# Each sample scored over its own 272 keys, latent queries over 128 rows, one copy and two tile turns at other places

## What is computed

```python
q_lat = jnp.einsum('bthn,rhn->bthr', q_nope, w_uk)
o_lat = mla_attend(q_lat, q_rope,
                   jnp.concatenate([ckv_past, ckv_new], axis=1),
                   jnp.concatenate([krope_past, kr_new], axis=1), None)
# in mla_attend: s = (q_lat . ckv + q_rope . krope) * ATTN_SCALE; p = softmax(s); p @ ckv
```

## Time and profile before

| | us |
|---|---|
| median of 3 runs | 776.85 (776.73 to 777.43) |
| the profiled execution | 776.64 |
| its span, first to last instruction | 774.8 |
| PE busy | 761.0 (98%), 3767 matrix instructions |
| DVE busy | 565.1 (73%) |
| ACT busy | 422.4 (55%) |
| POOL busy | 65.3 (8%) |
| chain that ended last | PE 90%, DVE 5%, ACT 3%, issue 1% |

### The profile page before, as it was taken

How to read it: one execution, slowest core, us unless ns; L and a number is a source line. 1 busy time by engine, 2 the same in 40 slices (tenths; PEclk the granted TensorE clock), 3 DMA queues, 4 the chain that set the end, 5 groups by cost and what they waited for, 6 DMA issues and landing times.

```text
span 774.8 us, 10544 instructions
## 1 busy us (share of the span) xinstructions
PE 761.0 (98%) x3767; PEld 605.5 (78%) x3767; DVE 565.1 (73%) x1092; ACT 422.4 (55%) x982; POOL 65.3 (8%) x114
## 2 busy tenths in 40 slices
PE   8999999999999999999999999999999999999995
PEld 7899877777777588888888988787777766888874
DVE  3459989877877985636463799898778789656477
ACT  3865656764446743263365485557544558223564
POOL 1400123210000400000000010232000000000000
PEclk9999999999999999999999999999999999999998
DMA  8822222100000353412281322221000005341203
GB/s 269 257 77 82 83 71 85 39 29 27 2 27 17 97 200 125 134 56 82 59 280 52 99 81 77 66 59 28 28 27 28 1 28 176 96 136 59 87 19 136
DMA packets 45833, 65.54 MB, mean 85 GB/s; under 512 B 12590, under 2 KB 24714, under 8 KB 45766
## 3 DMA queue, kind: packets, MB, share of 16 engines
q1 hardware_dynamic: 41946, 58.45, 24.0%
q0 software_dynamic: 3776, 6.40, 2.9%
q10 hardware_dynamic: 60, 0.02, 0.0%
HBM read 57.87 MB, written 7.18 MB: 84 GB/s over the span
## 4 chain that ended last, share of the span: by engine, by line
PE 90%; DVE 5%; ACT 3%; issue 1%; POOL 0%; DVEq 0%; ACTq 0%; POOLq 0%
PE acc L660 19%; PE acc L666 19%; PE acc L663 19%; PE sharedT L584 5%; PE acc L796 4%; PE sharedS L871 4%; PE sharedO L885 4%; PE sharedT L858 3%; PE sharedO L584 2%; PE sharedS L584 2%; PE sharedS L844 1%; PE sharedS L845 1%; PE sharedO L832 1%; DVE H L1804 1%; PE sharedS L852 1%
## 5 line engine op out<-in xcount | busy, mean ns | idle before, releaser
L660 PE MATMUL acc<-WHI,XHI 128*128 128x512 f32 (+1 forms) x710 | 309.2, 435 | 1.0 <-ACT WHI L1051 0.5
L666 PE MATMUL acc<-WHI,XLO 128*128 128x512 f32 (+1 forms) x710 | 274.6, 387 | 0.0
L663 PE MATMUL acc<-WLO,XHI 128*128 128x512 f32 (+1 forms) x710 | 274.3, 386 | 0.3 <-DVE WLO L1475 0.3
L1545 DVE SCALAR_TENSOR_TENSOR VT<-UX,CWT,VT 128x640 f32<-128x640 f32 x240 | 211.4, 882 | 4.6
L660 PEld LDWEIGHTS acc<-WHI,XHI 128*128 128x128 f32 x710 | 133.7, 188 | 33.0 <-issue 8.1
L663 PEld LDWEIGHTS acc<-WLO,XHI 128*128 128x128 f32 x710 | 133.9, 189 | 30.5 <-issue 8.1
L1475 DVE SCALAR_TENSOR_TENSOR WLO<-WR,GT,WHI 128x512 fp32r<-128x512 f32 (+1 forms) x142 | 98.6, 736 | 78.6 <-ACT WHI L1051 77.7
L666 PEld LDWEIGHTS acc<-WHI,XLO 128*128 128x128 f32 x710 | 133.3, 188 | 26.1
L1051 ACT ACTIVATE WHI<-WR,GT 128x512 fp32r<-128x512 f32 (+1 forms) x142 | 93.4, 709 | 91.3 <-PE acc L666 91.1
L1267 ACT ACTIVATE SB<-SB,NBIAS 128x384 f32<-128x384 f32 (+1 forms) x80 | 46.0, 574 | 39.7 <-DVE NBIAS L1599 39.1
L1051 ACT ACTIVATE PT<-sharedT 128x384 f32<-128x384 f32 (+1 forms) x80 | 35.7, 447 | 44.1 <-PE sharedT L584 43.2
(11 more groups left out here) (204 smaller groups left out, 872.5 us busy)
## 6 DMA issues: line engine op xcount, KB each, us to landing
WR<-in_w_in_dram SPq DMA_DIRECT2D x32, 256.0 KB, 3.1
WR<-in_w_in_dram SPq DMA_DIRECT2D x16, 512.0 KB, 3.6
WR<-in_w_out_dram SPq DMA_DIRECT2D x16, 512.0 KB, 3.7
WR<-in_w_pg_dram SPq DMA_DIRECT2D x16, 512.0 KB, 3.6
H<-in_x_prompt_dram SPq DMA_DIRECT2D x16, 256.0 KB, 5.0
WR<-in_w_in_dram SPq DMA_DIRECT2D x8, 416.0 KB, 3.8
residual_spill<-H SPq DMA_DIRECT2D x5, 512.0 KB, 4.3
H<-residual_spill SPq DMA_DIRECT2D x10, 256.0 KB, 3.3
```

The source lines that it names most:

```text
L660: mm(out, hi, w_hi, start=(first and k == 0), stop=False)
L663: mm(out, hi, w_lo, start=False, stop=False)
L666: last = mm(out, lo, w_hi, start=False, stop=(final and k == 1))
L1545: stt(out=out, in0=src, scalar=w, in1=out, op0=ALU.mult, op1=ALU.add).then_inc(conv_done, 1)
```

## The change

The code of the following engines is changed; removed lines begin with a minus. What it does:

- The 16 new keys of a sample follow right behind its cached ones. The cached keys are written to `CTK` at column 16 s instead of 0, so that columns 16 s to 16 s + 271 are the sample's 272 keys. The scores, the mask (now all zeros, by the helper of the units), the exponential and the sum go over 272 columns.
- The turned third piece holds the last 128 of the 272 columns. Its partner is a new tile `ZN`, zero except for its last 16 rows, which are the sample's own new rows. POOL clears `ZN` once and fills it in each layer by eight small transfers, issued as soon as the latents are ready; TensorE waits for them ahead of the first sample's third value product.
- The latent queries go over all 128 rows; POOL clears rows 64 to 127 of `UKT` in each layer, in layer 1 after a wait for the norm of layer 0, and TensorE waits for it.
- For sample 0 ScalarE copies the turned probabilities ahead of the convolution inputs instead of behind them.
- At the start the second tile's turn moves into the first half product, between its first product and the wait for the low part of the weights; one zero product less is made ahead of it.
- Two taps of the convolution move from samples 2 and 4 to units 22 and 23.

```diff
+KEYS = PAST + NS
 PLE = 256
...
 for _n in range(NB):
-    TAP[_n] = _take((4, 4, 5, 4, 5, 4, 4, 4)[_n])
+    TAP[_n] = _take(4)
 TAP["turn"] = _take(2)
-for _u, _m in enumerate((1, 1, 1, 3, 1, 1, 2, 2, 1, 1, 1, 3, 1, 1, 3, 2, 1, 1, 1, 3, 1, 1, 1, 1, 2, 1, 1, 2)):
+for _u, _m in enumerate((1, 1, 1, 3, 1, 1, 2, 2, 1, 1, 1, 3, 1, 1, 3, 2, 1, 1, 1, 3, 1, 1, 2, 2, 2, 1, 1, 2)):
     TAP[NB + _u] = _take(_m)
...
-        SMASK = sb("SMASK", [P, 3, 240], BF16)
+        ZN = sb("ZN", [P, NB, LORA])
         JUNK = sb("JUNK", [P, D], BF16)
...
         sums_in = sem("sums_in")
+        uk_cleared = sem("uk_cleared")
+        new_rows_in = sem("new_rows_in")
         conv_done = sem("conv_done")
...
+                        pe.wait_ge(x_in[0][1], 16)
+                        flip_half((0, ("x", 1, 0)), H[:, 1, :])
                         pe.wait_ge(first_lo, 1)
...
                 pe.wait_ge(warm_set, 1)
-                zeros(8)
+                zeros(7)
                 pe.wait_ge(ident_in, 16)
...
                         _, t, g = step
+                        if (t, g) == (1, 0):
+                            continue
                         pe.wait_ge(x_in[g][t], 16)
...
                 copied_wait(pe, (l, f"qs{g}"))
+                pe.wait_ge(uk_cleared, l + 1)
                 for j in range(4):
-                    last = mm(quad(name)[:, j, :], UKT[0:NOPE, 4 * g + j, :], QS[0:NOPE, :, 4 * g + j, :],
-                              start=True, stop=True)
+                    last = mm(quad(name)[:, j, :], UKT[:, 4 * g + j, :], QS[:, :, 4 * g + j, :], start=True, stop=True)
                 fill_inc(last, (l, name))
...
                 fill_wait(pe, (l, name))
-                for j in range(w // P):
-                    last = flip(quad(name)[:, j, :], SB[:, n % 2, P * j:P * (j + 1)])
+                for j, end in enumerate(range(P, w + P, P)):
+                    end = min(end, w)
+                    last = flip(quad(name)[:, j, :], SB[:, n % 2, end - P:end])
                 fill_inc(last, (l, name))
...
                     mm(out, CKV[:, s % CACHED, j, :], PT[:, s % 2, j, :], start=(j == 0), stop=False)
-                fill_inc(mm(out, Z[:, TILES - 1, QLORA:QLORA + LORA], PT[:, s % 2, 2, :],
-                            start=False, stop=True), (l, name))
+                if s == 0:
+                    pe.wait_ge(new_rows_in, 16 * NB * (l + 1))
+                fill_inc(mm(out, ZN[:, s, :], PT[:, s % 2, 2, :], start=False, stop=True), (l, name))
...
                 q_rot = QS[:, s, :, :].rearrange("p h t -> p (h t)")
-                mm(out[:, 0:PAST + P], q_lat, CTK[:, 0, :], start=True, stop=False)
-                fill_inc(mm(out[:, 0:PAST + P], q_rot, CTK[:, 1, :], start=False, stop=True), (l, name))
+                own = slice(NS * s, NS * s + KEYS)
+                mm(out[:, 0:KEYS], q_lat, CTK[:, 0, own], start=True, stop=False)
+                fill_inc(mm(out[:, 0:KEYS], q_rot, CTK[:, 1, own], start=False, stop=True), (l, name))
...
                 pe.wait_ge(exped, EXPS * l + s + 1)
-                flip_probs(s, PAST + P)
+                flip_probs(s, KEYS)
...
                 filled_wait(act, (l, name))
-                copy(CTK[:, 0, 0:PAST], bank((l, name))[:, 0:PAST])
+                at = NS * s
+                copy(CTK[:, 0, at:at + PAST], bank((l, name))[:, 0:PAST])
                 for j in range(2):
-                    out = copy(CTK[NOPE:P, 1, P * j:P * (j + 1)], quad(name)[NOPE * j:NOPE * (j + 1), 2, :])
+                    out = copy(CTK[NOPE:P, 1, at + P * j:at + P * (j + 1)], quad(name)[NOPE * j:NOPE * (j + 1), 2, :])
                 drain_inc(out, (l, name))
...
             for s in range(NB):
-                probs(s, PAST + P)
+                probs(s, KEYS)
                 if s:
...
                     value_rows_out(1)
-                if s in (NB - 3, NB - 2):
+                if s in (0, NB - 3, NB - 2):
...
                     block_out(s)
+                    if s == 0:
+                        turned_u_out(2, (s,))
                 else:
...
                     block_out(s)
-                    if s in (0, 1):
+                    if s == 1:
                         turned_u_out(2, (s,))
...
-            def sample_mask(s):
-                name = ("s", s)
-                filled_wait(dve, (l, name))
-                first = 112 - NS * s
-                drain_inc(nc.vector.tensor_tensor_reduce(
-                    SB[:, s % 2, 0:PAST + P].rearrange("p (j k) -> p j k", k=P),
-                    bank((l, name))[:, 0:PAST + P].rearrange("p (j k) -> p j k", k=P),
-                    SMASK[:, :, first:first + P], -SCALE, 3e38, ALU.add, ALU.min, NBIAS[:, s:s + 1]), (l, name))
...
-            sample_mask(0)
+            mask(0, KEYS, MASK[:, 0:KEYS])
             for s in range(NB):
                 if s < NB - 1:
-                    sample_mask(s + 1)
+                    mask(s + 1, KEYS, MASK[:, 0:KEYS])
                     taps(s)
...
             nc.gpsimd.memset(UX[:, :, 1, 0:STATE - NS], 0.0).then_inc(const_set, 1)
-            nc.gpsimd.memset(SMASK[:, 0:2, :], 0.0).then_inc(const_set, 1)
-            nc.gpsimd.memset(SMASK[:, 2, 0:112], NEG).then_inc(const_set, 1)
-            nc.gpsimd.memset(SMASK[:, 2, 112:128], 0.0).then_inc(const_set, 1)
-            nc.gpsimd.memset(SMASK[:, 2, 128:240], NEG).then_inc(const_set, 1)
             nc.gpsimd.memset(CTK[0:NOPE, 1, :], 0.0).then_inc(const_set, 1)
             nc.gpsimd.memset(MASK[:, :], 0.0).then_inc(const_set, 1)
-            pool.wait_ge(const_set, 8)
+            nc.gpsimd.memset(ZN[:, :, :], 0.0).then_inc(const_set, 1)
+            pool.wait_ge(const_set, 5)
             nc.gpsimd.memset(MASK[0:P // 2, 512 - P // 2:512], NEG).then_inc(const_set, 1)
...
+            if l:
+                pool.wait_ge(ln_done, TILES * l)
+            nc.gpsimd.memset(UKT[NOPE:P, :, :], 0.0).then_inc(uk_cleared, 1)
             pool.wait_ge(latents_ready, l + 1)
+            for s in range(NB):
+                pool.dma_start(ZN[P - NS:P, s, :], Z[NS * s:NS * (s + 1), TILES - 1, QLORA:QLORA + LORA]).then_inc(new_rows_in, 16)
             for name, col, n in (("new_ckv", QLORA, LORA), ("new_krope", NZ - ROPE, ROPE)):
...
                                Z[:, 0:4, col:col + n]).then_inc(latents_stored, 16)
...
```

More of the change, by code:

```diff
@@ L904, in tensor_layer @@
                 pe.wait_ge(tables_in, 16 * 2)
-                pe.wait_ge(const_set, 9)
+                pe.wait_ge(const_set, 6)
             for t in range(TILES):
@@ L1193, in first_tap @@
                 if l == 0:
-                    act.wait_ge(const_set, 9)
+                    act.wait_ge(const_set, 6)
                 out = VTv[:, :, c, :].rearrange("p t (b j) -> p t b j", j=NS)
@@ L1548, in vector_layer @@
             if l == 0:
-                dve.wait_ge(const_set, 9)
+                dve.wait_ge(const_set, 6)
             low(first_i + 6)
```

## The result

The changed kernel takes 772.39 us (median of 4 runs, 772.19 to 773.10) where the kernel before takes 776.98: a ratio of 0.9941, 95% interval 0.9925 to 0.9956. That is 4.6 us faster; forecast were 5.6 us and 771.2 us, with a range of 769.9 to 773.8. The profiled execution took 772.29 us, its span went from 774.8 to 770.5.

A forecast was written before the change was run, and what follows sets the result against it. TensorE was taken as the bound, busy in 98% of the span. Start -0.9, samples and latent queries -5.4, taps +0.7 give -5.6 us: 776.85 to 771.2 us; own range 769.9 to 772.2, with rivals 1 and 3 to 773.8.

The forecast's parts named there:

- Scores over 272 columns: Each score product takes about 0.457 us, 0.188 us less; 3.0 us a layer, 6.0 us in all before waits.
- Latent queries and the first mask: 128 rows save 0.36 us a layer; a new 0.3 us wait for VectorE's first mask swallows nearly all of it.
- the mask's end at 111.86: Ahead of the second sample's scores: PE, there at 111.62, waits for the mask and goes on at about 111.93.
- The copy: ScalarE's new order gives nothing; the first sample's values still wait for the last `UX` copy, 1.0 us instead of 0.62.
- The taps: Two taps moved into units 22 and 23 cost 0.33 us a layer, 0.7 in all; bounds zero and 0.8 a layer.
- rival 3: VectorE becomes the bound and both moved taps land on the path: +2.5 us, 773.7 us; chance 0.14.
- The start: Second tile's earlier turn and one zero product less save 0.9 us together, with bounds 0 and 1.1.
- no slack at all: At the start the second tile's input lands at 7.13, just as PE's stream is free from 7.14; nearly no loss expected.
- rival 1: The start gives nothing, as the input lands later than 7.13 or the fast clock comes later: 772.1 us; chance 0.12.
- Layer 1's samples: Samples with latent queries save 2.69 us in layer 1, the same as in layer 0.
- two layers 5.4: One layer's saving of 0.81 + 1.88 = 2.69 us taken twice; bounds 2.4 and 3.7 us a layer.
- The part on POOL: Eight `ZN` issues, 3.86 us, fit into POOL's 4.95 us wait and cost nothing; without that cover 0.48 us each.

The follow-up runs named there:

- Wide scores: Score products read and write all 384 columns again, the mask takes its 272 out of them, all else as changed: 776.35 us, ratio 0.9993 to the kernel before.
- later inputs: Changed kernel with the third quarter's turned inputs of the first two samples moved behind the values and one more filler product group: 770.43 us, ratio 0.9917.
- early rotary rows: Changed kernel with GpSimd loading a later sample's rotary cache rows once the replaced rows are turned, not after that sample's values: 772.50 us, ratio 0.9941.
- two taps at other places: Changed kernel with one tap moved from unit 23 to 22 and one from unit 24 to 26: 770.30 us, ratio 0.9916.

## Why the prediction was right or wrong

- **Scores over 272 columns: right.** 0.46 us a product; v0-v7 fell by 39.16 - 37.32 = 1.84 us (1.88 forecast). Wide scores put it back to 39.19.
- **Latent queries and the first mask: right.** 1.94 us, and the new wait on the mask, with 0.31 us lost, swallows nearly all of it. With 64 rows the kernel was no slower. The step of the prediction that set this against the mask's end at 111.86 held; without it the sum would have been 0.6 us too good. By v0 the layer had 0.71 us of the forecast 0.81.
- **The copy: right.** 0.90 us of waiting for `UX`, 1.0 forecast; the new order gives 0.09 us a layer, where the forecast had nothing. Bank O's order decides, not which record is named: L847 named `UX` in one order and `PT` in the other for the same wait. The later inputs took the wait away by giving the bank another order.
- **The taps: right.** 0.31 and 0.35 us against 0.33, and the old taps give back as much. VectorE's room in the samples (rival 3's point) was there: no mask of samples 2 to 7 was waited for.
- **The start: term too large.** 0.51 us in the profiled pair instead of 0.9. The step that failed is that the landing of the second tile at 7.13 and PE's first product at 6.91, both of one execution, were taken as if they were fixed. In the profile after they came at 7.53 and 7.10, the latter because PE's pace rose only at 7.13 and not at 4.54; each alone would have put the second tile's first product near 9.65, against the 9.37 of the forecast. About 0.1 us was wrong in the path itself: even from 6.91 the product would have come at 6.91 + 2.57 = 9.48. The prediction called the landing "no slack at all" and yet kept the full gain; the bounds of 0 and 1.1 and rival 1, with both of its conditions, had the case. With a late landing the early turn gives nothing.
- **Layer 1's samples: term too large by 0.6 to 0.8.** -1.90 us instead of -2.69. The step that failed is "two layers 5.4", one layer worked out and doubled. The part on POOL weighed only what the change adds there (the `ZN` issues) and not who stands at its deadline: a sample's cache load, three issues and 2.4 us of flight behind the values. The sample period fell from 5.36 us (125.60 to 130.96) to 4.99 (124.03 to 129.02), and in layer 1 a delay of POOL of 1.2 us no longer fitted in. The prediction couldn't know this delay: in the trace of before it was 0.48 us and at another load.

The two misses, 0.4 and 0.8 us, and 0.1 us in layer 0's samples make the 1.3 us between the forecast 5.6 and the 4.3 us of span. The direction was reasoned; that the range held is in part luck. 772.39 lies above the forecast's own range (769.9 to 772.2) and close to rival 1's 772.1, but the start gave half of its gain, and the larger miss is the delay in layer 1, which no rival had. It fell into the room that the range had for rivals 1 and 3.

## What to carry to other kernels

When a change shortens a loop's period, work out for every transfer that is issued from inside the loop whether it still meets the next turn; a queue with slack before is the next wait after. A gain that hangs on one landing time, or on the moment at which TensorE's pace rises, needs more than one execution's number for it. And the few waits that the list of the bound engine names may be worth more than work taken off it: another place for five turns a layer and another for two taps, with no work saved, gave 2 us each here, together as much as 32 narrower products.

## What the runs showed of the hardware

- The same load, issued at 2.6 us in every execution, landed 4.2 to 5.0 us later in nine profiles and 5.9 to 6.0 in five, with nothing between. It is one of the first loads of the program; from 3 to 8 us the DMA share is 0.84 to 1.09 in the profile after. What parts the two groups stays open.
- POOL's issue stream stops once in layer 1, for about 1.2 us, between the cache loads: in the profile after ahead of the load at 501.82, in the kernel before at 506.25 with 0.48 us seen, with the early rotary rows at 498.24 with 0.95. "issue" means that nothing in the profile explains it. In all 13 profiles of the changed kernel and its variants, the one with wide scores too, it stands ahead of POOL's 97th DMA issue, at times between 491 and 506; in the kernel before it stands ahead of the 83rd. From 486.6 to 505 the profile after has no load of instructions among its DMA packets. Its cause stays open.

```profile
498.24 1.45 POOL L511 DMA_DIRECT2D CKR<-in_cache_krope_dram  x2 [0.95 <-issue]
```

- At the start PE's passes of 128 columns take 0.21 us each and then 0.11, as at its two levels of 1.2 and 2.4 GHz. PE had been busy without a gap since 1.11 us, but the place of the rise differs between executions of the same code: the clock records begin at 3.99 to 7.13 in the 14 profiles (7.13 and 4.27 for the changed kernel), and no view shows the slow level ahead of them. Where the rise came at 6.5 or later and the landing early, PE's first product at 7.10, and not the load, set the second tile's first product: with a landing at 6.83 (two taps at other places) it still came at 9.68.
